# A mixture-of-experts trunk: expert outputs go to DRAM by slot and are fetched per token, in place of products with the slot matrix

## The chip, the cores and the metric

The kernel runs on one core of one Trainium2 chip. The metric is the device time of one execution, in microseconds (us). The kernel before took 1487.02 us, the median of 3 runs (1486.68 to 1487.57).

## The reference, cut to what matters

A two-layer trunk: 256 tokens of width 1024, attention and a dense SwiGLU in layer 0, attention and a mixture of 8 experts in layer 1. The change is in the mixture alone:

```python
logits = (t @ w_router).astype(jnp.float32)
top_val, top_idx = lax.top_k(logits, TOP_K)              # TOP_K = 2
gates = jax.nn.softmax(top_val, axis=-1)
combine = jnp.sum(jax.nn.one_hot(top_idx, N_EXPERTS, dtype=jnp.float32) * gates[..., None], axis=1)
y = jnp.zeros_like(t)
for e in range(N_EXPERTS):                                # N_EXPERTS = 8, EXPERT_FF = 3584
    y = y + combine[:, e:e + 1].astype(t.dtype) * swiglu(t, w_gate_up[e], w_down[e])
```

A token needs only its two experts. Everything is float32 in and out.

## The kernel before, in words

**Precision.** Every float32 product on TensorE (PE) is done as three products of rounded parts: high by high, high by low, low by high (`product`, L1665 to L1667). So each weight unit of 1 MB (128 partitions by 2048 values) is read from DRAM by SyncE's queue (SP) into one of six buffers `raw`. ScalarE (ACT) rounds it into `whi` (`split_hi`, L612), VectorE (DVE) subtracts to get `wlo` (`split_lo`, L975). `whi` and `wlo` have three places each: ACT may write unit c only when PE has finished unit c-3, and a load waits until DVE has finished the unit six before it.

**An expert** has 42 units in 7 steps of 512 columns. In step j PE does two G units (gate), two U units (up), and the two D units (down) of step j-1. One unit is 12 matmuls of 128x512. Between G's first and second unit PE transposes the previous step's activations (L2206); they pass through banks 6 and 7, which ACT and DVE read out. Banks 0 and 1 collect the down products of an expert over all 7 steps, banks 2 to 5 hold gate and up sums. Expert 0 and expert 7 are written out, experts 1 to 6 are one loop on every engine. Four units of expert 7 are loaded early into spare tiles (`attn`, `tok`).

**Tokens by slot.** Each expert has 128 slots. DVE builds the slot matrix `slot_oh` (token by slot, one_hot, L1531). For experts 1 to 7 PE gets the slots' token numbers from it, GpSimd's queue (POOL) fetches these rows from a copy `hn_rows` in DRAM with an indirect DMA (L586) during the previous expert, and PE transposes them (L2143).

**The way back.** In step 1 of each expert PE transposes the slot matrix (L2237) and ACT copies it to `slot_ohT` (L931). When the expert is done, that is in step 0 of the next one, ACT copies banks 0 and 1 to `ye_hi` (`output_hi`, L892), DVE makes `ye_lo` (`output_lo`, L1541), PE multiplies by `slot_ohT` (`back`, L2119 and L2120: 8 matmuls of 128x512, four after the first U unit, four after the second), and DVE adds the four results to the residual `X`, scaled by each token's gate (`add_back`, L1555). After expert 7 the same is done once more, in the open.

There is a second pass (`ps` = 1) for the case that more than 128 tokens choose one expert. It is skipped by a branch when, as here, it isn't needed.

The order is written out by hand for each engine. A wait that isn't met holds all later work of that engine.

Of the kernel before, what the change touches and what calls it, by code (L numbers as in the profile page):

```python
# [19 lines left out]
P = 128  # L20
# [47 lines left out]
TB = len(TB_USES)  # L68

# [108 lines left out]
def tb_count(use):  # L178

    return TB_USES.index(use) + 1  # L180


def tb_bank(use):
    return 6 + tb_count(use) % 2
# [6 lines left out]
def build(nc, x, mem, positions, mix_norm_g, ffn_norm_g, mem_norm_g, w_mem_kv, w_out, w_in_a, b_forget, w_q_b,  # L191
          lambda_q1, lambda_k1, lambda_q2, lambda_k2, subln_g, kv_norm_g, w_kv_shared, w_gate_up_dense,
          w_down_dense, w_router, w_gate_up_moe, w_down_moe, final_norm_g, out):
    with ExitStack() as ctx:
# [99 lines left out]
        xg_rows = hn[:, 0, :]  # L294
# [66 lines left out]
        hn_saved = sem("hn_saved")  # L361
        rows_ready, rows_out, rows_in = sem("rows_ready"), sem("rows_out"), sem("rows_in")
# [142 lines left out]
        def _(pool):  # L505
# [78 lines left out]
            for e in range(1, N_EXP):  # L584
                pool.wait_ge(rows_out, e)
                pool.indirect_dma_start(xg_rows, None, hn_rows,  # L586
                                        bass.IndirectOffsetOnAxis(ap=row_of[:, 0:1], axis=0)).then_inc(rows_in, 16)


        @block.scalar  # L590
        def _(act):
# [284 lines left out]
            def experts_act(ps):  # L876
                ub = U_MOE + ps * N_EXP * MOE_UNITS
                tb = 2 + TB * N_EXP * ps
                hb = FFN_STEPS + MOE_STEPS * N_EXP * ps

                def halves(use, base, dst, done):

                    for i in range(2):
                        act.wait_ge(tb_ready, base + tb_count(f"{use}{i}"))
                        a.copy(dst[:, 4 * i:4 * i + 4, :],
                               bank[tb_bank(f"{use}{i}")][:].rearrange("p (c n) -> p c n", c=4)).then_inc(done, 1)

                def output_hi(e):

                    act.wait_ge(unit_used, ub + MOE_UNITS * e)  # L890
                    for i in range(2):
                        a.copy(ye_hi[:, 4 * i:4 * i + 4, :],  # L892
                               bank[i][:].rearrange("p (c n) -> p c n", c=4)).then_inc(ye_hi_ready, 1)

                def expert(e, turns, first=False, final=False):
# [6 lines left out]
                    def evac_T(j):  # L902
                        act.wait_ge(tb_ready, tb + TB * e + tb_count(f"T{j}") - (2 if final and j == MOE_STEPS - 1 else 0))
                        a.copy(h2T_hi[j % 2][:], bank[tb_bank(f"T{j}")][:]).then_inc(h2_hi, 1)  # L904
# [8 lines left out]
                    if not first:  # L913
                        output_hi(e)
# [4 lines left out]
                    for j in range(1, MOE_STEPS):  # L919
# [9 lines left out]
                        if j == 1:  # L929
                            act.wait_ge(tb_ready, tb + TB * e + tb_count("oneT"))  # L930
                            a.copy(slot_ohT[:], bank[tb_bank("oneT")][:, 0:SEQ]).then_inc(ohT_out, 1)  # L931
                    if not final:
                        halves("gather", tb + TB * e, xg_hi, xg_hi_ready)
# [5 lines left out]
                halves("gather", tb - tb_count("gather1"), xg_hi, xg_hi_ready)  # L939
# [21 lines left out]
        def _(dve):  # L961
# [542 lines left out]
            def combine_weights():  # L1504
# [11 lines left out]
                step(ins)  # L1516
                step(d.tensor_reduce(over[:, 0:1], bank[4][:, 64:64 + N_EXP], AX.X, ALU.max))
# [3 lines left out]
            def experts_dve(ps):  # L1521
                ub = U_MOE + ps * N_EXP * MOE_UNITS
                tb = 2 + TB * N_EXP * ps
                hb = FFN_STEPS + MOE_STEPS * N_EXP * ps
                xb = 2 * N_EXP * ps
                ab = 4 + 4 * N_EXP * ps
# [9 lines left out]
                def halves(use, count, hi, lo, ready, done):  # L1536

                    for i in range(2):
                        dve.wait_ge(ready, count + i + 1)
                        b = bank[tb_bank(f"gather{i}")] if use == "gather" else bank[i]  # L1540
# [3 lines left out]
                def output_lo(e):  # L1544

                    halves("output", 2 * (N_EXP * ps + e) - 2, ye_hi, ye_lo, ye_hi_ready, ye_lo_ready)

                def add_back(e, i):
# [3 lines left out]
                    dve.wait_ge(tb_ready, tb + TB * e - TB + tb_count(f"back{i}")  # L1552
                                - (2 if isinstance(e, int) and e == N_EXP else 0))
                    dve.wait_ge(x_added, ab + 4 * e - 4)
                    d.scalar_tensor_tensor(out=X[:, t, cols], in0=bank[tb_bank(f"back{i}")][:],  # L1555
                                           scalar=comb[:, t, bass.ds(e - 1, 1)], in1=X[:, t, cols],
                                           op0=ALU.mult, op1=ALU.add).then_inc(x_added, 1)

                def expert(e, turns, first=False, final=False):
# [6 lines left out]
                    def evac_T(j):  # L1566
                        dve.wait_ge(h2_hi, hb + MOE_STEPS * e + j + 1)
                        d.tensor_tensor(h2T_lo[j % 2][:], bank[tb_bank(f"T{j}")][:], h2T_hi[j % 2][:].bitcast(F32),
                                        ALU.subtract).then_inc(h2_lo, 1)

                    def mul(j):
# [3 lines left out]
                        if j >= 2:  # L1575
                            dve.wait_ge(tb_ready, tb + TB * e + tb_count(f"T{j - 2}"))
                        elif not first:
                            dve.wait_ge(tb_ready, tb + TB * e - TB + tb_count("T6"))
# [5 lines left out]
                    if not first:  # L1584
# [3 lines left out]
                    if not first:  # L1588
# [3 lines left out]
                    if not first:  # L1592
# [14 lines left out]

# [681 lines left out]
```

## Time and profile before

| | |
|---|---|
| runs | 1486.68, 1487.02, 1487.57 us |
| the profiled execution, own time | 1487.61 us |
| its span, first to last instruction | 1485.7 us |
| PE busy | 1440.2 us (97%) |
| DVE busy | 1177.9 us (79%) |
| ACT busy | 952.1 us (64%) |
| mean granted TensorE clock | 0.989 of 2.4 GHz |
| moved by DMA | 432.61 MB, 291 GB/s over the span |
| chain that ended last | PE 91%, DVE 5%, issue 1%, ACT 1% |

The experts take the part from about 485 us to 1472 us. A busy time of PE is the union of its matmuls, and a matmul's own duration overlaps that of the next one, since they are pipelined. What one matmul costs in a row of them is the distance between two starts. "Idle before" is the time in which the engine had nothing running before the group, with what ended it.

### The profile page before, as it was taken

Reading aid. Unit: us, or ns where it says so; the run is one execution under the profiler, and the core shown is the slowest. Engines: PE = TensorE matmul, PEld = TensorE weight load, DVE = VectorE, ACT = ScalarE, POOL = GpSimd, SP = SyncE. Lnnn points to the kernel's source line nnn. Section 1 sums busy time; section 2 is a strip of 40 time slices with the busy share of each in tenths; the row PEclk is TensorE's granted clock in tenths of the full one; section 3 lists DMA queues with packets and bytes.
Section 4 is the critical chain, followed back from the end, with each engine's and each line's share of the span. In section 5 each row is a group of like instructions: output and inputs, shape, how many; then the busy total and the mean of one; then the engine's idle time right before and its main releaser. Section 6 shows DMA issues by size and latency. Waiting matters only on the chain.

```text
span 1485.7 us, 20701 instructions
## 1 busy us (share of the span) xinstructions
PE 1440.2 (97%) x7727; PEld 1222.5 (82%) x7727; DVE 1177.9 (79%) x1053; ACT 952.1 (64%) x876; POOL 27.6 (2%) x59
## 2 busy tenths in 40 slices
PE   8999999999998999999999999999999999999995
PEld 6987999998887788788888878878888887887884
DVE  6675444547787798988988898898889888889885
ACT  5545343335466577777767767777777777777774
POOL 2000000000000000000000000000000000000000
PEclk9999999999999899999999999999999999999998
DMA  9644355564534799999999999999999999998891
GB/s 303 200 129 156 129 170 179 191 202 150 171 114 174 284 379 381 338 361 380 376 338 387 374 334 378 383 335 369 391 365 342 375 376 340 371 390 294 312 375 51
DMA packets 205195, 432.61 MB, mean 291 GB/s; under 512 B 7008, under 2 KB 54112, under 8 KB 205136
## 3 DMA queue, kind: packets, MB, share of 16 engines
q1 hardware_dynamic: 202592, 423.65, 79.7%
q0 software_dynamic: 2544, 8.16, 1.7%
q8 instruction: 38, 0.62, 0.2%
q14 instruction: 21, 0.17, 0.0%
HBM read 429.69 MB, written 2.10 MB: 291 GB/s over the span
## 4 chain that ended last, share of the span: by engine, by line
PE 91%; DVE 5%; issue 1%; ACT 1%; DMA 0%; DVEq 0%; ACTq 0%; POOLq 0%
PE bank L1665 28%; PE bank L1667 28%; PE bank L1666 28%; DVE wlo L975 3%; PE bank L2206 1%; DVE X L1555 1%; PE bank L1680 1%; PE bank L1948 1%; PE bank L2119 0%; PE bank L1784 0%; PE bank L2120 0%; PE bank L2143 0%; PE bank L1822 0%; PE bank L1803 0%; PE bank L1848 0%
## 5 line engine op out<-in xcount | busy, mean ns | idle before, releaser
L975 DVE TENSOR_TENSOR wlo<-raw,whi 128x2048 fp32r<-128x2048 f32 x397 | 907.8, 2290 | 176.7 <-ACT whi L612 175.2
L612 ACT CAST whi<-raw 128x2048 fp32r<-128x2048 f32 x397 | 758.2, 1915 | 210.3 <-PE bank L1667 210.3
L1665 PE MATMUL bank<-whi,op_hi 128*128 128x512 f32 (+1 forms) x1176 | 444.0, 378 | 7.8 <-DVE wlo L975 4.6
L1667 PE MATMUL bank<-whi,op_lo 128*128 128x512 f32 (+1 forms) x1176 | 435.4, 370 | 0.0
L1666 PE MATMUL bank<-wlo,op_hi 128*128 128x512 f32 (+1 forms) x1176 | 435.1, 370 | 0.0
L1665 PEld LDWEIGHTS bank<-whi,op_hi 128*128 128x128 f32 x1176 | 222.1, 189 | 51.3 <-DVE wlo L975 9.9
L1667 PEld LDWEIGHTS bank<-whi,op_lo 128*128 128x128 f32 x1176 | 221.9, 189 | 38.6
L1666 PEld LDWEIGHTS bank<-wlo,op_hi 128*128 128x128 f32 x1176 | 222.3, 189 | 35.4
L1665 PE MATMUL bank<-whi,h2T_hi 128*128 128x512 f32 x544 | 214.3, 394 | 1.0 <-DVE h2T_lo L1371 1.0
L1667 PE MATMUL bank<-whi,h2T_lo 128*128 128x512 f32 x544 | 212.1, 390 | 0.0
L1666 PE MATMUL bank<-wlo,h2T_hi 128*128 128x512 f32 x544 | 211.9, 389 | 0.0
L1665 PE MATMUL bank<-op_hi,whi 128*128 128x256 f32 x512 | 148.0, 289 | 3.0 <-DVE wlo L975 3.0
L1666 PE MATMUL bank<-op_lo,whi 128*128 128x256 f32 x512 | 146.9, 287 | 0.0
L1667 PE MATMUL bank<-op_hi,wlo 128*128 128x256 f32 x512 | 146.8, 287 | 0.0
L1667 PEld LDWEIGHTS bank<-whi,h2T_lo 128*128 128x128 f32 x544 | 102.1, 188 | 21.7
L1665 PEld LDWEIGHTS bank<-whi,h2T_hi 128*128 128x128 f32 x544 | 102.2, 188 | 21.5 <-DVE h2T_lo L1371 1.4
L1666 PEld LDWEIGHTS bank<-wlo,h2T_hi 128*128 128x128 f32 x544 | 102.2, 188 | 20.2
L1665 PEld LDWEIGHTS bank<-op_hi,whi 128*128 128x128 f32 x512 | 100.5, 196 | 5.1 <-DVE wlo L975 3.2
L1666 PEld LDWEIGHTS bank<-op_lo,whi 128*128 128x128 f32 x512 | 100.5, 196 | 0.4
L1667 PEld LDWEIGHTS bank<-op_hi,wlo 128*128 128x128 f32 x512 | 100.3, 196 | 0.0
L904 ACT CAST h2T_hi<-bank 128x512 fp32r<-128x512 f32 x56 | 32.9, 587 | 72.8 <-PE bank L2206 72.8
L804 ACT ACTIVATE prob<-bank 128x512 f32<-128x512 f32 x11 | 6.6, 597 | 87.3 <-PE bank L1667 87.3
(297 smaller groups left out, 854.2 us busy)
## 6 DMA issues: line engine op xcount, KB each, us to landing
raw<-in_w_gate_up_moe_dram SPq DMA_DIRECT2D x223, 1024.0 KB, 6.8
raw<-in_w_down_moe_dram SPq DMA_DIRECT2D x109, 1024.0 KB, 7.0
raw<-in_w_gate_up_dense_dram SPq DMA_DIRECT2D x22, 1024.0 KB, 5.2
raw<-in_w_down_dense_dram SPq DMA_DIRECT2D x11, 1024.0 KB, 5.0
raw<-in_w_in_a_dram SPq DMA_DIRECT2D x10, 1024.0 KB, 13.1
raw<-in_w_out_dram SPq DMA_DIRECT2D x8, 1024.0 KB, 5.1
raw<-in_w_kv_shared_dram SPq DMA_DIRECT2D x6, 1024.0 KB, 5.2
raw<-in_w_mem_kv_dram SPq DMA_DIRECT2D x4, 1024.0 KB, 6.3
```

The lines of the kernel that those rows point to most:

```text
L612: a.copy(whi[:, c % SPLIT, :], src).then_inc(hi_ready, 1)
L804: a.activation(gate_act[j % 2][:], bank[4 + 2 * (j % 2)][:], ACT.Silu).then_inc(silu_done, 1)
L904: a.copy(h2T_hi[j % 2][:], bank[tb_bank(f"T{j}")][:]).then_inc(h2_hi, 1)
L975: d.tensor_tensor(wlo[:, c % SPLIT, :], src, whi[:, c % SPLIT, :].bitcast(F32), ALU.subtract).then_inc(lo_ready, 1)
L1555: d.scalar_tensor_tensor(out=X[:, t, cols], in0=bank[tb_bank(f"back{i}")][:], scalar=comb[:, t, bass.ds(e - 1, 1)], in1=X[:, t, cols], op0 ...
L1665: m.matmul(dst, sh, mh, start=start and i == 0, stop=False)
L1666: m.matmul(dst, sh, ml, start=False, stop=False)
L1667: last = m.matmul(dst, sl, mh, start=False, stop=stop and i == n - 1)
L1680: last = m.transpose(bank[g][:, P * c:P * (c + 1)], hn[:, t, P * k:P * (k + 1)], ident[:])
L1948: m.matmul(bank[4 + 2 * n + h][:], ones_row, gain_row[n][:, 512 * h:512 * (h + 1)], start=True, stop=True).then_inc(gain_out, 1)
L2206: last = m.transpose(bank[tb_bank(f"T{j}")][:, P * c:P * (c + 1)], h2[j % 2][:, P * c:P * (c + 1)], ident[:])
```

## The change

Experts 0 to 6 no longer go back through PE. ACT copies banks 0 and 1 as they are into a row tile `ye_rows` (the half `hn[:, 1, :]`), and POOL's queue writes it to DRAM at `y_rows`, 128 rows of 4 KB for each expert. The routing computes for each token and each of its two choices a row number, expert * 128 + slot, and a share, the gate. Where the choice is expert 7, or lies beyond slot 128, both are zero. During expert 7 two pairs of indirect DMAs fetch each token's first and then its second row into `hn`, and DVE adds them to `X` with the shares, in steps 2 and 4 (`add_stored`, two operations of 128x1024 each). Expert 7's own rows still go back by the products. The diff runs through POOL, ACT, the routing and the experts on DVE, and PE, in this order. The transposes of the slot matrix stay for expert 7 alone, now in its last step. The second pass keeps the old way.

```diff
             for e in range(1, N_EXP):
                 pool.wait_ge(rows_out, e)
                 pool.indirect_dma_start(xg_rows, None, hn_rows,
                                         bass.IndirectOffsetOnAxis(ap=row_of[:, 0:1], axis=0)).then_inc(rows_in, 16)
+                pool.wait_ge(y_out, 2 * e)
+                pool.dma_start(y_rows[P * (e - 1):P * e, :], ye_rows).then_inc(hn_saved, 16)
+            pool.wait_ge(hn_saved, 16 * (NT + N_EXP - 1))
+            pool.wait_ge(route_ready, 1)
+            pool.wait_ge(xg_lo_ready, 2 * N_EXP)
+            for i in range(2):
+                if i:
+                    pool.wait_ge(x_added, 4 + NT)
+                for t in range(NT):
+                    pool.indirect_dma_start(hn[:, t, :], None, y_rows,
+                                            bass.IndirectOffsetOnAxis(ap=back_of[:, i, t:t + 1],
+                                                                      axis=0)).then_inc(back_in, 16)
...
+                def output_rows(e):
+                    act.wait_ge(unit_used, ub + MOE_UNITS * e)
+                    act.wait_ge(hn_saved, 16 * e + 16 * (NT - 1))
+                    for i in range(2):
+                        a.copy(ye_rows[:, 512 * i:512 * (i + 1)], bank[i][:]).then_inc(y_out, 1)
...
                     if not first:
-                        output_hi(e)
+                        if ps:
+                            output_hi(e)
+                        else:
+                            output_rows(e)
...
+                for i in range(2):
+                    ins = d.tensor_tensor(place[:, i], oh[:, i], rank[:, :, 0:N_EXP], ALU.mult)
+                step(ins)
+                chosen = top_f[:, :, 0:2].rearrange("p t i -> p i t")
+                step(d.tensor_reduce(slot_of[:], place[:], AX.X, ALU.add))
+                step(d.tensor_scalar(known[:], slot_of[:], float(P), None, ALU.is_lt))
+                step(d.scalar_tensor_tensor(out=known[:], in0=chosen, scalar=float(N_EXP - 1), in1=known[:],
+                                            op0=ALU.is_lt, op1=ALU.mult))
+                step(d.scalar_tensor_tensor(out=slot_of[:], in0=chosen, scalar=float(P), in1=slot_of[:],
+                                            op0=ALU.mult, op1=ALU.add))
+                step(d.tensor_tensor(slot_of[:], slot_of[:], known[:], ALU.mult))
+                d.tensor_copy(back_of[:], slot_of[:])
+                d.tensor_tensor(share[:], gates[:, :, 2:4].rearrange("p t i -> p i t"), known[:], ALU.mult)
...
+                def add_stored(i):
+                    dve.wait_ge(back_in, 16 * NT * (i + 1))
+                    dve.wait_ge(x_added, 4 + NT * i)
+                    for t in range(NT):
+                        d.scalar_tensor_tensor(out=X[:, t, :], in0=hn[:, t, :], scalar=share[:, i, t:t + 1],
+                                               in1=X[:, t, :], op0=ALU.mult, op1=ALU.add).then_inc(x_added, 1)
...
-                    if not first:
+                    if ps and not first:
                         output_lo(e)
                     lo("U", 0, 0)
                     lo("U", 0, 1)
-                    if not first:
+                    if ps and not first:
                         add_back(e, 0)
                         add_back(e, 1)
...
+                        if j in (2, 4) and final and not ps:
+                            add_stored(j // 2 - 1)
                         lo("D", j - 1, 0)
...
                         up("U", j, 0)
-                        if j == 0 and not first:
+                        if j == 0 and ps and not first:
                             back(e, (0, 1))
                         up("U", j, 1)
-                        if j == 0 and not first:
+                        if j == 0 and ps and not first:
                             back(e, (2, 3))
-                        if j == 1:
-                            for t in range(NT):
-                                last = m.transpose(bank[tb_bank("oneT")][:, P * t:P * (t + 1)],
-                                                   slot_oh[:, t, :].bitcast(F32), ident[:])
-                            last.then_inc(tb_ready, 1)
+                        if j == 1 and ps or j == MOE_STEPS - 1 and final and not ps:
+                            one_hot_transposes()
...
+                        if j == 1 and not ps and not first:
+                            pe.wait_ge(y_out, 2 * e)
                         if j:
                             down(j - 1, 0)
```

**VectorE at the start of experts 1 to 6.** In the kernel before its queue holds this from `output_lo` on (`wlo<-raw,whi` is one weight unit's `split_lo`; register rows cost nothing to speak of):

```order
L1541 TENSOR_TENSOR op_lo<-bank,op_hi 128x4x128 [waits ye_hi_ready] x2
L973 REGISTER_ALU
L975 TENSOR_TENSOR wlo<-raw,whi 128x2048 [waits hi_ready]
L973 REGISTER_ALU
L975 TENSOR_TENSOR wlo<-raw,whi 128x2048 [waits hi_ready]
L1552 ISA
L1554 REGISTER_ALU [waits tb_ready]
L1555 ISA [waits x_added]
L1555 SCALAR_TENSOR_TENSOR X<-bank,comb,X 128x512
L1555 SCALAR_TENSOR_TENSOR X<-bank,comb,X 128x512 [waits x_added,tb_ready]
L973 REGISTER_ALU
L975 TENSOR_TENSOR wlo<-raw,whi 128x2048 [waits hi_ready]
```

In the changed kernel the same place, from the second weight unit of the expert on, reads (L1033 is `split_lo`, L1659 the product of gate and up):

```order
L1033 TENSOR_TENSOR wlo<-raw,whi 128x2048 [waits hi_ready]
L1031 REGISTER_ALU
L1033 TENSOR_TENSOR wlo<-raw,whi 128x2048 [waits hi_ready]
L1031 REGISTER_ALU
L1033 TENSOR_TENSOR wlo<-raw,whi 128x2048 [waits hi_ready]
L1031 REGISTER_ALU
L1033 TENSOR_TENSOR wlo<-raw,whi 128x2048 [waits hi_ready]
L1652 ISA
L1653 REGISTER_ALU [waits unit_used]
L1658 ISA [waits silu_done]
L1659 TENSOR_TENSOR probT<-prob,bank 128x512 [waits tb_ready]
```

Two subtractions and four additions into `X` have left this stretch, and with them the waits for PE's products (tb_ready) between two weight units.

**VectorE in step 2 of expert 7.** The changed kernel has two new rows between a U unit and the D units:

```order
L1033 TENSOR_TENSOR wlo<-raw,whi 128x2048 [waits hi_ready] x3
L1648 TENSOR_TENSOR h2T_lo<-bank,h2T_hi 128x512 [waits h2_hi]
L1033 TENSOR_TENSOR wlo<-raw,whi 128x2048 [waits hi_ready]
L1636 SCALAR_TENSOR_TENSOR X<-hn,share,X 128x1024 [waits x_added,back_in]
L1636 SCALAR_TENSOR_TENSOR X<-hn,share,X 128x1024
L1033 TENSOR_TENSOR wlo<-attn,whi 128x2048 [waits hi_ready]
L1033 TENSOR_TENSOR wlo<-raw,whi 128x2048 [waits hi_ready]
L1659 TENSOR_TENSOR probT<-prob,bank 128x512 [waits tb_ready,silu_done,unit_used]
```

Before, the D unit in `attn` follows the U unit at once. The same pair stands once more in step 4.

**TensorE in step 0 of experts 1 to 6.** Before, between the last matmul of one U unit and the first of the next:

```order
L1667 MATMUL bank<-whi,op_lo 128x512
L2119 MATMUL bank<-op_hi,slot_ohT 128x512 [waits xg_lo_ready,ohT_out,ye_lo_ready]
L2120 MATMUL bank<-op_lo,slot_ohT 128x512
L2119 MATMUL bank<-op_hi,slot_ohT 128x512 [waits h2_lo]
L2120 MATMUL bank<-op_lo,slot_ohT 128x512
L2169 REGISTER_ALU
L1665 MATMUL bank<-whi,op_hi 128x512 [waits lo_ready]
```

In the changed kernel the four L2119 and L2120 rows are gone here and after the second U unit.

## Rows read from the trace of the kernel before

**Rows 1.** Windows: length, PE, PEld, DVE, ACT, POOL busy, clock, DMA share, GB/s.

```profile
510.00:600.00 90.00, 90.00 (x410) 74.47 (x409) 80.26 (x47) 67.33 (x45) 2.97 (x1) 1.00 1.02 379
700.00:725.00 25.00, 25.00 (x118) 20.77 (x117) 21.90 (x12) 18.52 (x15) 0.97 (x1) 1.00 1.04 396
740.00:862.00 122.00, 121.33 (x553) 99.81 (x552) 109.30 (x68) 89.24 (x62) 0.94 (x1) 1.00 1.00 365
```

**Rows 2.** Groups by line, PE, 500 to 1480 us: busy, mean ns, idle before.

```profile
L2119 PE MATMUL bank<-op_hi,slot_ohT 128*128 128x512 f32 x32 | 12.8, 400 | 2.4 <-DVE op_lo L1541 2.0 <-DVE X L1555 0.4
L2120 PE MATMUL bank<-op_lo,slot_ohT 128*128 128x512 f32 x32 | 12.5, 390 | 0.0
```

**Rows 3.** Timeline of PE, step 0 of expert 3: start us, us, instruction.

```profile
863.04 0.50 PE L1665 MATMUL bank<-whi,op_hi 128*128 128x512 f32 x1
...
865.93 0.39 PE L2119 MATMUL bank<-op_hi,slot_ohT 128*128 128x512 f32 x1
...
866.84 0.39 PE L1665 MATMUL bank<-whi,op_hi 128*128 128x512 f32 x1
...
869.56 0.39 PE L2119 MATMUL bank<-op_hi,slot_ohT 128*128 128x512 f32 x1
...
870.47 0.50 PE L1665 MATMUL bank<-whi,op_hi 128*128 128x512 f32 x1
...
873.33 0.60 PE L2206 MATMUL bank<-ident,probT 128*128 128x128 f32 x4
874.60 0.50 PE L1665 MATMUL bank<-whi,op_hi 128*128 128x512 f32 x1 [0.67 <-DVE wlo L975]
874.94 0.40 PE L1666 MATMUL bank<-wlo,op_hi 128*128 128x512 f32 x1
```

**Rows 4.** Timeline of PE, the same place in expert 0.

```profile
507.80 0.60 PE L2206 MATMUL bank<-ident,probT 128*128 128x128 f32 x4
...
508.56 0.39 PE L1666 MATMUL bank<-wlo,op_hi 128*128 128x512 f32 x1
```

**Rows 5.** Timeline of PE, slot matrix transposes in expert 7.

```profile
1371.11 0.39 PE L1667 MATMUL bank<-whi,op_lo 128*128 128x512 f32 x1
...
1371.80 0.39 PE L1666 MATMUL bank<-wlo,h2T_hi 128*128 128x512 f32 x1
```

**Rows 6.** Timeline of DVE, step 0 of expert 3.

```profile
860.69 4.49 DVE L975 TENSOR_TENSOR wlo<-raw,whi 128x2048 fp32r<-128x2048 f32 x2 [0.20 <-ACT whi L612]
866.80 1.41 DVE L1555 SCALAR_TENSOR_TENSOR X<-bank,comb,X 128x512 f32<-128x512 f32 x2 [1.62 <-PE bank L2120]
...
870.34 1.41 DVE L1555 SCALAR_TENSOR_TENSOR X<-bank,comb,X 128x512 f32<-128x512 f32 x2
...
872.26 4.49 DVE L975 TENSOR_TENSOR wlo<-raw,whi 128x2048 fp32r<-128x2048 f32 x2
```

**Rows 7.** Timelines of DVE and PE, step 2 of expert 7.

```profile
1385.17 2.29 DVE L975 TENSOR_TENSOR wlo<-attn,whi 128x2048 fp32r<-128x2048 f32 x1
...
1388.41 0.39 PE L1665 MATMUL bank<-whi,h2T_hi 128*128 128x512 f32 x1
```

**Rows 8.** Groups by line, DVE: the nearest operations to the new ones.

```profile
L1499 DVE TENSOR_TENSOR op_lo<-hn,op_hi 128x1024 fp32r<-128x1024 f32 x1 | 1.2, 1219 | 0.0
...
L1653 DVE SCALAR_TENSOR_TENSOR hn<-X,stat,gain 128x512 f32<-128x512 f32 x2 | 1.4, 747 | 0.0
```

**Rows 9.** Timeline of DVE, expert 0's fourth unit, first after the routing.

```profile
499.11 2.29 DVE L975 TENSOR_TENSOR wlo<-raw,whi 128x2048 fp32r<-128x2048 f32 x1 [1.05 <-ACT whi L612]
```

**Rows 10.** DMA issues: KB each, median us to landing.

```profile
hn_rows<-hn POOLq DMA_DIRECT2D x2, 512.0 KB, 7.2
...
hn<-hn_rows,row_of POOLq DMA_INDIRECT x7, 7.1
```

**Rows 11.** Weight loads (L430), 620 to 1350 us.

```profile
DMA to landing us min/median/max: 5.0/7.0/9.4
```

**Rows 12.** Waits of ACT in expert 3: us in total, times, longest.

```profile
ACT whi L612 <- PE bank L1667: 20.4, 31, 1.7
```

More of the change, by code:

```diff
@@ L68 @@
 TB = len(TB_USES)
+TB_USES0 = [f"T{j}" for j in range(6)] + ["gather0", "gather1", "T6"]
+TB0 = len(TB_USES0)
+TB_PASS0 = 2 + TB0 * N_EXP - 2 + 5
 FILL = list(np.cumsum([4, 4, 8, 4, 4, 8, 5, 4]))
@@ L175, in moe_pos, with tb_start, tb_turn, tb_count @@
     return base + 2 * (kind == "U") + a
[L178 to L184, printed above, removed]
+def tb_start(ps):
+    return 2 + TB_PASS0 * ps
+def tb_turn(ps):
+    return TB if ps else TB0
+def tb_count(ps, use, final=False):
+    if ps:
+        return TB_USES.index(use) + 1 - 2 * (final and (use == "T6" or use[:4] == "back"))
+    if use[:4] == "back":
+        return TB0 + int(use[4])
+    if use == "oneT":
+        return TB_USES0.index("gather0") + 1
+    return TB_USES0.index(use) + 1 - (final and use == "T6")
+def tb_bank(ps, use):
+    if ps:
+        return 6 + tb_count(1, use) % 2
+    if use[:4] == "back":
+        return 7 - int(use[4]) % 2
+    return 6 if use == "oneT" else 6 + int(use[-1]) % 2
 S1, R1 = N0, N0
@@ L293, in build @@
         hn_rows = nc.dram_tensor("hn_rows", (SEQ, D), F32).ap()
-        xg_rows = hn[:, 0, :]
+        xg_rows, ye_rows = hn[:, 0, :], hn[:, 1, :]
+        y_rows = nc.dram_tensor("y_rows", ((N_EXP - 1) * P, D), F32).ap()
+        place = sb("place", [P, 2, NT, N_EXP])
+        slot_of = sb("slot_of", [P, 2, NT])
+        known = sb("known", [P, 2, NT])
+        share = sb("share", [P, 2, NT])
+        back_of = sb("back_of", [P, 2, NT], I32)
         over = sb("over", [P, 2])
@@ L902, in evac_T @@
                     def evac_T(j):
-                        act.wait_ge(tb_ready, tb + TB * e + tb_count(f"T{j}") - (2 if final and j == MOE_STEPS - 1 else 0))
-                        a.copy(h2T_hi[j % 2][:], bank[tb_bank(f"T{j}")][:]).then_inc(h2_hi, 1)
+                        act.wait_ge(tb_ready, tb + turn * e + tb_count(ps, f"T{j}", final))
+                        a.copy(h2T_hi[j % 2][:], bank[tb_bank(ps, f"T{j}")][:]).then_inc(h2_hi, 1)
                     def silu(j):
@@ L928, in expert @@
                         hi("D", j - 1, 1)
-                        if j == 1:
-                            act.wait_ge(tb_ready, tb + TB * e + tb_count("oneT"))
-                            a.copy(slot_ohT[:], bank[tb_bank("oneT")][:, 0:SEQ]).then_inc(ohT_out, 1)
+                        if j == 1 and ps:
+                            one_hot_T(e)
                     if not final:
-                        halves("gather", tb + TB * e, xg_hi, xg_hi_ready)
+                        halves("gather", tb + turn * e, xg_hi, xg_hi_ready)
+                    elif not ps:
+                        one_hot_T(e)
                     hi("D", MOE_STEPS - 1, 0)
@@ L1591, in expert @@
                     lo("G", 1, 0)
-                    if not first:
+                    if ps and not first:
                         add_back(e, 2)
@@ L2193, in h2_transposes @@
                         pe.wait_ge(mul_done, hb + MOE_STEPS * e + j + 1)
[L2195 removed]
+                        if j == MOE_STEPS - 1 and not ps:
+                            pe.wait_ge(*((ohT_out, 1) if final else (xg_lo_ready, xb + 2 * e + 3)))
+                        elif not ps:
+                            pe.wait_ge(h2_lo, hb + MOE_STEPS * e + max(j - 1, 0))
+                        elif j == 0:
                             pe.wait_ge(x_added, ab + 4 * e)
                         elif j == 2:
[L2198 removed]
+                            pe.wait_ge(ohT_out, yb + e + 1)
                         elif j == MOE_STEPS - 1 and final:
```

67 lines of the change are left out of this document (38 added, 29 removed).

## The prediction, written before the changed kernel ran

> **What bounds the kernel now.** I read the windows first. Inside the experts PE is busy for 121.3 of 122 us at full granted clock, while DVE has 109.3, ACT 89.2 [rows 1]. So PE's order sets the time there, and work taken off PE is worth its full price, as long as DVE, ACT and the loads keep ahead. Next I read the groups by line, to find what leaves PE: 32 L2119 and 32 L2120, with a mean of 400 and 390 ns [rows 2]. This mean must not be used as a price. The timeline shows that four such matmuls take from 865.93 to 866.84, 0.91 us, so one costs 0.2275 us; the rest of its 0.39 overlaps the next one [rows 3]. Last I read the timelines at the start of an expert, since the change works there. DVE has more to do in that place than anywhere else: two subtractions, and four additions to X that wait for PE's products, 1.62 us idle in one go [rows 6]. It falls behind, and PE pays: the unit after the transposes starts late with 0.67 us idle [rows 3].
>
> **What leaves PE.** (a) The products of `back` for experts 0 to 6: 7 experts x 8 matmuls x 0.2275 = 12.7 us. Those of expert 7 stay. They stand between full units with no gap before or behind [rows 3], so all of it is on the path. (b) The transposes of the slot matrix: eight pairs become one. From the last product before the pair to the second behind it are 0.69 us [rows 5], where three steps without a pair would have only two distances, 0.455; a pair costs 0.235 us, 7 of them 1.7 us.
>
> **What leaves DVE, and so PE's wait.** Step 0 loses two subtractions, four additions and the wait between them. In expert 3 DVE's two units from 860.69 are done at 865.18. The third begins only after the wait and two additions, at 868.2, and after two more additions and a product the fourth begins at 872.26 [rows 6]. PE needs the third at 870.47 and gets it just then: that unit takes 2.86 us up to 873.33, where the one between 866.84 and 869.56 takes 2.72, so 0.14 us are lost. It needs the fourth after the transposes. From their start to the second matmul behind them are 1.61 us [rows 3]. Expert 0 has the same step with no way back in it, and there the distance is 0.76 us [rows 4]. That is a direct look at the changed order: 0.85 us go. Together 0.99 us an expert, and 6.9 us for seven. What is late next in this place? The unit before the first products is 2.89 us long (865.93 less 863.04, from the same timeline's start of that unit), because ACT's two copies of banks 0 and 1 stand before its cast. These copies remain, with another target, so this 0.15 us stays. After it ACT, not DVE, is the later one, and PE has its unit in time.
>
> **What is added to DVE in expert 7.** Two pairs of additions of 128x1024. The trace has none of that shape. A multiply-add of 128x512 takes 0.747 us, a subtraction of 128x1024 1.22 us [rows 8]; two of 128x512 back to back take 1.41 [rows 6]. Going by width, the two bounds are 2 x 1.22 = 2.44 and 4 x 0.705 = 2.82 us for a pair; I take 2.5, nearest to the row of full width. They stand in front of the D unit in `attn`. Before, this one is done at 1385.17 + 2.29 = 1387.46, and PE begins on it at 1388.41 [rows 7]: a lead of 0.95 us. With 2.5 us in front it is 1.55 us late. The lead comes back by itself before the next unit, since DVE needs 2.3 us for one and PE 2.72. So each pair costs PE about 1.6 us, the two 3.2 us. Bounds: 2.44 - 0.95 = 1.5 and 2.82 - 0.95 + some 0.3 us of semaphore and start = 2.2 a pair; and nothing below, if the lead in steps 2 and 4 were larger, which the rows don't show. So 0 to 4.4, I take 3.2.
>
> **What is added and hidden.** (c) The routing gets nine small operations on DVE; at 0.2 us each for those with a step behind them, some 1.6 us. The next unit's subtraction waits 1.05 us for ACT there before [rows 9], and PE has three units to work on, the first ones at a lower clock. I count 0, at most 0.55. (d) ACT writes two copies to another place: 0; one copy of `slot_ohT` an expert goes. (e) POOL gets seven stores and four fetches. A store of 512 KB took 7.2 us to land, an indirect fetch of the same size 7.1 [rows 10]. Rows are ready some 1.3 us after expert 7 starts, so the store lands at +9 and the first two fetches at about +18. DVE asks for them at about +36 (step 2). The second pair is asked for 34 us after the first, and needs some 10. Both are covered by 18 us or more; if a cover were gone, each us late would be one us of PE, because the additions hold DVE's queue. POOL has nothing else queued behind them. (f) PE's new wait for `y_out` before the first D unit concerns copies that were done a step earlier: 0. ACT's wait for the previous store is met an expert earlier: 0.
>
> **The loads.** Each expert now also writes 0.52 MB. Per 122 us the core moves 122 x 365 = 44.5 MB; it would be 45.05 MB in about 119 us, 379 GB/s. Is that to be had? Over 90 us of expert 0 and 1 it moved 379, over 25 us 396 [rows 1]. A load lands 5.0 to 9.4 us after its issue [rows 11], and ACT's cast never waits for one: its 20.4 us of waiting in an expert are for PE [rows 12]. Six buffers at 2.72 us, less the 1.5 units that ACT is ahead of DVE, leave some 12 us from issue to use, 3 more than the worst landing. A store adds 0.52 / 0.39 = 1.3 us to the landing of the units beside it. So I count 0, but this is the thinnest cover in the sum.
>
> On this the Trainium skill speaks against the change. "DMA: Bandwidth & Descriptors", section "Where 436 GB/s comes from", puts the HBM side at about 358 GB/s for one core and says that this side binds transfers between HBM and SBUF. By that rule the experts would be bound by memory already, and any added byte would be time. The trace doesn't agree: 365 GB/s over a whole expert and 396 over 25 us [rows 1].
>
> **The sum.** 12.7 + 1.7 + 6.9 - 3.2 = 18.1 us. The profiled execution's own time was 1487.61 us, of which the span is 1485.7; both fall by it, to 1469.5 and 1467.6. The median of the runs was 0.6 us lower than the profiled execution, so I predict 1469.0 us. The tail after expert 7 has the same work in the same order as before, and nothing is taken from it.
>
> **Rivals.**
> 1. *The loads become the bound.* The mechanism: DMA can't sustain more than the 365 GB/s that a whole expert shows. Then an expert takes 45.05 / 0.365 = 123.4 us in place of 122, in all of experts 0 to 6, 7 x 1.4 = 10 us slower: 1497 us. It decides from the point where the sustained rate is below 45.05 MB / 122 us = 369 GB/s. For it: DMA share is 1.00 or above in all three windows. Against it: 379 and 396 GB/s in two of them, with the same share, so the share doesn't tell that the engines are full [rows 1]; and no cast waits for a load. A rate between 369 and 379 would give back a part only, 1470 to 1487. 7 in 100 for both, 5 of these slower.
> 2. *Another engine is late in the same place.* The removal of `back` gives PE 1.8 us less to do while ACT still copies banks 0 and 1. If ACT's casts are then the last, the 0.99 us of waiting stays and the pair costs its upper bound: 12.7 + 1.7 - 4.4 = 10.0, 1477 us. For it: the 0.15 us that ACT already costs. Against it: expert 0's distance [rows 4], though there ACT has no copies to do. 14 in 100.
> 3. *The stored rows come too late.* If the fetch of 128 single rows takes several times the 7.1 us, or POOL's queue is held, DVE and PE stop in step 2. With 18 us of cover it would need a threefold time to cost anything, and 18 us more than the cover to cancel the gain: about 1480 if it is 11 us late. 3 in 100.
> 4. *The additions are hidden.* The lead of DVE recovers enough, or the pair is faster, and the 3.2 us aren't paid: 1466 us. 12 in 100.
>
> The forecast as it stands has 64 in 100, with its own range of 1467 to 1471.5. Within 0.2% (3 us, what a measurement of this kernel can tell from no change) of before lies only a thin part of rival 1. So faster 0.93, same 0.02, slower 0.05. The range from 1465.0 to 1476.0 leaves out rival 1, most of rival 3 and a part of rival 2.
>
> **What would show it.** Right: L2119-like products appear only 8 times after 500 us; the distance over the transposes in step 0 is 0.76 us in every expert; an expert's period is 119.1 us, 3 less; PE's waits for `wlo` at starts of experts are gone, and two new ones of about 1.6 us stand in expert 7 behind the pairs of 128x1024. Wrong: casts of ACT that wait for a DMA, a period above 121 us, or DVE waiting for a fetch in expert 7. If the period is right and only the end is off, the additions were mis-sized.

## The result, and the profile after

The changed kernel takes 1471.59 us, the median of 4 runs (1468.94 to 1471.91). The kernel before took 1487.04 us beside it (4 runs, 1486.68 to 1487.57). The ratio is 0.9888, with a 95% interval from 0.9876 to 0.9900: 15.4 us faster. The forecast was 1469.0 us, within 1465.0 to 1476.0. The profiled execution took 1471.91 us, where the sum gave 1469.5.

The page of the changed kernel, the span and the busy time of each engine:

```profile
span 1470.0 us, 20457 instructions
PE 1424.3 (97%) x7657; PEld 1210.9 (82%) x7657; DVE 1156.0 (79%) x1024; ACT 949.9 (65%) x869; POOL 40.0 (3%) x70
```

PE's busy time fell by 15.9 us (from 1440.2) and the span by 15.7. This looks as if only products had gone, and that would be a wrong reading: busy time hides PE's short waits. The transposes below count as 0.60 us busy whether the next unit starts 0.61 us after them, as here, or 0.35 us, as in d1 further down. So each part is read from distances.

PE at the start of expert 3, the place of [rows 3]. Units are counted as in the prediction, from the first U unit on. The rows are the first matmul of the second and of the third unit, the transposes, and the first two matmuls of the fourth unit.

```profile
861.21 0.39 PE L1747 MATMUL bank<-whi,op_hi 128*128 128x512 f32 x1
863.93 0.39 PE L1747 MATMUL bank<-whi,op_hi 128*128 128x512 f32 x1
866.65 0.60 PE L2299 MATMUL bank<-ident,probT 128*128 128x128 f32 x4
867.26 0.50 PE L1747 MATMUL bank<-whi,op_hi 128*128 128x512 f32 x1
867.60 0.40 PE L1748 MATMUL bank<-wlo,op_hi 128*128 128x512 f32 x1
```

Two units of 2.72 us with nothing between, then 0.61 us from the transposes to the next unit and 0.95 us to its second matmul. In [rows 3] the latter was 1.61 us, and in [rows 4], the model for the forecast, 0.76. DVE in the same place:

```profile
855.99 6.70 DVE L1033 TENSOR_TENSOR wlo<-raw,whi 128x2048 fp32r<-128x2048 f32 x3 [1.47 <-ACT whi L654]
864.32 0.69 DVE L1659 TENSOR_TENSOR probT<-prob,bank 128x512 f32<-128x512 f32 x1 [1.63 <-PE bank L1749]
864.92 2.28 DVE L1033 TENSOR_TENSOR wlo<-raw,whi 128x2048 fp32r<-128x2048 f32 x1
```

Three units stand in a row, ahead of PE. Then DVE waits 1.63 us for PE's last U product before it can multiply gate and up (L1659), and only behind that comes the subtraction of the fourth unit. It starts at 864.92, ends at 867.20, and PE's fourth unit starts at 867.26. So PE still waits here for DVE, if far less than in [rows 3]. The wait shows in the row of the weight load:

```profile
867.26 0.19 PEld L1747 LDWEIGHTS bank<-whi,op_hi 128*128 128x128 f32 x1 [0.25 <-DVE wlo L1033]
```

A period is read from the fetches of rows, one an expert. POOL's timeline before, and then after:

```profile
1188.71 0.95 POOL L586 DMA_INDIRECT hn<-hn_rows,row_of  x1 [121.18 <-DVE row_of L1604]
1310.82 0.94 POOL L586 DMA_INDIRECT hn<-hn_rows,row_of  x1 [121.16 <-DVE row_of L1604]
```

```profile
1175.39 0.99 POOL L616 DMA_INDIRECT hn<-hn_rows,row_of  x1 [81.80 <-DVE row_of L1684]
1294.69 0.99 POOL L616 DMA_INDIRECT hn<-hn_rows,row_of  x1 [81.80 <-DVE row_of L1684]
1331.58 0.55 POOL L619 DMA_DIRECT2D y_rows<-hn  x1 [35.89 <-ACT hn L942]
1338.16 2.65 POOL L627 DMA_INDIRECT hn<-y_rows,back_of  x1 [6.04 <-DMA y_rows<-hn]
1341.11 0.97 POOL L627 DMA_INDIRECT hn<-y_rows,back_of  x1 [0.30 <-issue]
1368.65 2.75 POOL L627 DMA_INDIRECT hn<-y_rows,back_of  x1 [26.57 <-DVE X L1636]
```

The period falls from 122.11 to 119.30 us. The last store is issued at 1331.58, the first two fetches at 1338.16 and 1341.11. Their median landing by the page's list of DMA issues, after the store and the fetch of an expert's tokens:

```profile
y_rows<-hn POOLq DMA_DIRECT2D x7, 512.0 KB, 6.3
hn<-hn_rows,row_of POOLq DMA_INDIRECT x7, 7.6
hn<-y_rows,back_of POOLq DMA_INDIRECT x4, 7.3
```

So the first rows are there by 1349. DVE adds them in step 2 of expert 7:

```profile
1363.70 2.30 DVE L1033 TENSOR_TENSOR wlo<-raw,whi 128x2048 fp32r<-128x2048 f32 x1 [0.69 <-ACT whi L654]
1365.91 2.48 DVE L1636 SCALAR_TENSOR_TENSOR X<-hn,share,X 128x1024 f32<-128x1024 f32 x2
1368.30 2.29 DVE L1033 TENSOR_TENSOR wlo<-attn,whi 128x2048 fp32r<-128x2048 f32 x1
```

There is no wait before the additions, and 17 us of cover (1349 to 1366). They delay the D unit in `attn`, and PE waits for it:

```profile
1370.73 0.47 PE L1747 MATMUL bank<-whi,h2T_hi 128*128 128x512 f32 x1 [1.29 <-DVE wlo L1033]
```

The unit before it began at 1366.56. It had 4.17 us instead of 2.72, so 1.45 are lost, and some 0.1 more in its first distance. The second pair costs the same. After 500 us PE's products with `slot_ohT` are these eight, of expert 7, where [rows 2] has 32 and 32 (by line, from 500 us on):

```profile
L2201 PE MATMUL bank<-op_hi,slot_ohT 128*128 128x512 f32 x4 | 1.9, 474 | 2.4 <-DVE op_lo L1613 2.0 <-DVE X L1627 0.4
L2202 PE MATMUL bank<-op_lo,slot_ohT 128*128 128x512 f32 x4 | 1.6, 393 | 0.0
```

The window of one expert, with the columns of [rows 1]:

```profile
740.00:860.00 120.00, 119.99 (x546) 98.90 (x546) 106.20 (x62) 89.77 (x61) 1.54 (x2) 1.00 1.02 379
```

The loads move 379 GB/s over 120 us, where [rows 1] had 365 over a whole expert. The Trainium skill, "DMA: Bandwidth & Descriptors", section "Where 436 GB/s comes from", gives about 358 GB/s per core and says that this side binds transfers between HBM and SBUF. This chip moved more for the length of an expert, with one core at work, and the measurement decides.

### The profile page after: what moved, and what is told of

The parts are those of the page before. It is cut to its first block, busy times and chain, and to the rows that moved or that the text cites. A ratio compares the mean times of both kernels' runs of the same rounds, so it can differ in the third digit from the quotient of the medians.

```text
span 1470.0 us, 20457 instructions
## 1 busy us (share of the span) xinstructions
PE 1424.3 (97%) x7657; PEld 1210.9 (82%) x7657; DVE 1156.0 (79%) x1024; ACT 949.9 (65%) x869; POOL 40.0 (3%) x70
## 4 chain that ended last, share of the span: by engine, by line
PE 93%; DVE 4%; ACT 2%; issue 1%; DMA 0%; DVEq 0%; ACTq 0%; POOLq 0%
PE bank L1747 29%; PE bank L1749 29%; PE bank L1748 28%; PE bank L2299 2%; DVE wlo L1033 1%; ACT whi L654 1%; PE bank L1866 0%; PE bank L2225 0%; PE bank L1904 0%; PE bank L1885 0%; PE bank L1930 0%; PE bank L1871 0%; PE bank L2201 0%; DVE X L1636 0%; DVE op_lo L1103 0%
## 5 line engine op out<-in xcount | busy, mean ns | idle before, releaser
L1033 DVE TENSOR_TENSOR wlo<-raw,whi 128x2048 fp32r<-128x2048 f32 x397 | 907.1, 2290 | 178.7 <-ACT whi L654 177.4
```

What stands on the lines that cost most here:

```text
L1033: d.tensor_tensor(wlo[:, c % SPLIT, :], src, whi[:, c % SPLIT, :].bitcast(F32), ALU.subtract).then_inc(lo_ready, 1)
```

## The experiments

Executions differ by up to 3 us before the experts, where the change does nothing (last section). So besides the median this section uses a stretch of the profiled execution, one for each kernel: from the cast of the routing (`top_f`) to the memset of `over`, DVE's first operation behind the expert sums. This is "the expert stage". Its parts are the time to the first fetch, six periods, and the end. Between the two executions of the changed kernel no part differs by more than 0.3 us; the end is less steady in others (m1 and c1 below).

| run | median us | ratio to before, 95% | expert stage | period | last fetch to end |
|---|---|---|---|---|---|
| before | 1487.04 | 1 | 995.67 | 122.15 | 165.90 |
| changed | 1471.59 | 0.9888 (0.9876 to 0.9900) | 979.16 | 119.30 | 166.34 |
| a1 changed again | 1471.90 | 0.9897 (0.9880 to 0.9913) | 979.16 | 119.28 | 166.60 |
| d1 DVE's part alone | 1481.57 | 0.9956 (0.9940 to 0.9973) | 988.67 | 121.01 | 165.69 |
| p1 PE's part alone | 1485.66 | 0.9983 (0.9973 to 0.9992) | 993.28 | 121.77 | 165.65 |
| m1 one wait moved | 1471.01 | 0.9885 (0.9868 to 0.9901) | 979.41 | 119.14 | 167.64 |
| c1 copies split | 1469.37 | 0.9871 (0.9855 to 0.9887) | 978.08 | 119.06 | 166.98 |
| n1 no additions | 1468.07 | 0.9872 (0.9856 to 0.9889) | 976.02 | 119.31 | 163.40 |
| s1 additions in halves | 1466.84 | 0.9864 (0.9848 to 0.9881) | 976.15 | 119.32 | 163.36 |
| r1 three stores | 1470.54 | 0.9879 (0.9862 to 0.9895) | 979.12 | 119.30 | 166.36 |
| b1 three edits | 1466.25 | 0.9850 (0.9837 to 0.9863) | 973.81 | 118.87 | 163.64 |

Medians are of 4 runs each, b1's of 5 and p1's of 10. The kernel before had 1487.61 beside a1, m1, s1 and n1, 1487.86 beside d1, p1, r1 and c1, and 1487.75 beside b1. The seven fetches bound six periods. The column is the mean of the last five; the first is some 0.6 us shorter in every kernel. d1, p1 and n1 leave out or shrink work, as said below, so their output isn't that of the reference.

### The changed kernel again

> The changed kernel once more, as it is, so that the next three have it beside them on the same chip. The profiled execution of it spans 1470.0 us; 2.4 us of the forecast gain are missing. Theory A says 1.3 to 1.5 us of them sit in the start of experts 1 to 6 (2.83 us gained in each, in place of 3.05) and 0.8 us came before the experts, where the change does nothing and executions differ. So here the periods of the experts stay at 119.3 us, while the time before the experts may be up to 1 us different, and the median lies between 1469 and 1472 us.

Its expert stage is the same as the changed kernel's to 0.01 us, while the profiled execution is 2.8 us shorter (1469.14 against 1471.91). The whole difference lies before the experts, and it is more than the 1 us that was expected. So 1 or 2 us between two medians say nothing here, and the stage does.

### One wait of DVE's product moved (m1)

```diff
     def mul(j):
-        dve.wait_ge(unit_used, ub + moe_pos("U", j, 1) + 1 + MOE_UNITS * e)
         dve.wait_ge(silu_done, hb + MOE_STEPS * e + j + 1)
         ...
+        dve.wait_ge(unit_used, ub + moe_pos("U", j, 1) + 1 + MOE_UNITS * e)
         d.tensor_tensor(h2[j % 2][:], gate_act[j % 2][:], bank[3 + 2 * (j % 2)][:],
```

> The order of the three waits ahead of VectorE's product of gate and up is turned, so that the wait for TensorE's last up unit comes last. Theory A: in the looped experts register instructions stand between this wait and the product, and delay it by 0.19 us against expert 0, which is written out (0.61 us from the last matmul's start to the product, against 0.42); the fourth weight unit and with it TensorE is late by that in step 0. So the distance from the transposes in step 0 to the next matmul falls from 0.61 to 0.42 us in experts 1 to 6, the period from 119.3 to 119.1 us, and the time by 6 x 0.19 = 1.1 us. Rival: the 0.19 us come from ScalarE's copies earlier in the step; then nothing changes.

PE in step 0 of expert 3:

```profile
866.51 0.60 PE L2299 MATMUL bank<-ident,probT 128*128 128x128 f32 x4
866.94 0.50 PE L1747 MATMUL bank<-whi,op_hi 128*128 128x512 f32 x1
```

0.43 us, where the changed kernel has 0.61 and expert 0 has 0.42. The six periods together fell by 1.05 us, 0.17 each. The transposes were not late: they follow the matmul before them by 0.23 us in both kernels. Late was the unit behind them, since its subtraction stands in DVE's queue behind the product of gate and up. From the start of PE's last U matmul to that product are 0.62 us in the changed kernel and 0.43 in m1. In experts 1 to 6, which are a loop, the order has two instructions between the wait for PE and the product, L1653 (which carries that wait) and L1658. The views leave such rows out, but the trace file has them. L1653 starts at 864.14 and L1658 at 864.22, the product at 864.32. In m1 the two corresponding rows are done 3.1 us ahead of the product, while DVE waits. In expert 7, which is written out and has no such instructions there, the same edit makes the distance longer, 0.52 in place of 0.42, and in expert 0 0.49.

The 1.05 us of the six periods don't show in the stage, since its end took 1.3 us longer. Of these, 0.9 lie between the last unit's last matmul and the end of the last addition, where the granted clock was lower (last section); 0.3 lie in the idle time between the last addition and the memset.

### The additions in halves (s1) and not at all (n1)

```diff
-    if j in (2, 4) and final and not ps:
-        add_stored(j // 2 - 1)
+    if j in (2, 3, 5, 6) and final and not ps:
+        add_half(2 * (2, 3, 5, 6).index(j))         # 128x512, ahead of a U unit
     lo("U", j, 1)
     ...
     lo("D", j - 1, 0)
+    if j in (2, 3, 5, 6) and final and not ps:
+        add_half(2 * (2, 3, 5, 6).index(j) + 1)     # 128x512, ahead of a D unit
```

This is s1, in short; n1 drops the fetches and `add_stored`, with the waits that counted them.

> The four additions of 128x1024 in expert 7 are cut into eight of 128x512, one ahead of the second up unit and one behind the first down unit in each of steps 2, 3, 5 and 6. Theory A: TensorE pays only for what goes beyond VectorE's lead of 0.95 us and its own pauses of 0.4 to 0.7 us; an addition of 0.7 us fits in. So both waits of 1.3 to 1.6 us of TensorE in expert 7 go, and the time falls by 3.1 us (1.5 at least). Rival: what expert 7 lost comes from the fetches (their traffic, or GpSimd's queue) and not from the additions; then it stays, or spreads over four steps.

> Leaves out the fetch of the stored rows and their additions to X, so that only expert 7's rows reach the output; the stores remain. Theory A: the same time as with the additions cut in halves, 3.1 us less than the changed kernel, since fetches that land in time cost nothing. Rival: the fetches cost something of their own (more than 0.5 us below the kernel with halves).

The stage falls by 3.0 us in s1 and by 3.1 in n1. So spread in eight halves the additions cost nothing that shows, and in pairs they cost all that leaving them out would bring. The fetches cost nothing of their own that shows (0.1 us between the two). A half of s1, in expert 7:

```profile
1360.01 0.74 DVE L1645 SCALAR_TENSOR_TENSOR X<-hn,share,X 128x512 f32<-128x512 f32 x1
```

0.74 us fit into the idle time that DVE has before nearly every unit (0.42 or 0.69 us for ACT's cast) plus its lead of 0.95; the view of waits has none of PE from 1330 to 1445 us.

### Each part alone (d1, p1)

d1 is the kernel before without `output_lo` and the additions in step 0; the eight products stay, and PE's waits for what is left out are turned into waits that are met:

```diff
     lo("G", 0, 1)
-    if not first:
-        output_lo(e)
     lo("U", 0, 0)
     lo("U", 0, 1)
-    if not first:
-        add_back(e, 0)
-        add_back(e, 1)
     lo("G", 1, 0)
-    if not first:
-        add_back(e, 2)
-        add_back(e, 3)
     mul(0)
```

p1 is the kernel before with the eight products cut to two columns; all of DVE's work stays:

```diff
-    one_pass(bank[tb_bank(f"back{i}")][:].rearrange("p (c n) -> p c n", c=4), oneT, oneT,
-             ye_hi[:, 4 * h:4 * h + 4, :], ye_lo[:, 4 * h:4 * h + 4, :], True, True)
+    b = bank[tb_bank(f"back{i}")]
+    one_pass(b[:, 0:2], oneT, oneT, ye_hi[:, 4 * h, 0:2], ye_lo[:, 4 * h, 0:2], True, True)
```

> The kernel before, with VectorE's part of the way back left out for experts 0 to 6 (the subtractions to ye_lo and the additions to X; their rows don't reach the output), while TensorE still does all its products. Theory A: this alone removes TensorE's wait for the fourth weight unit in step 0, 0.85 + 0.14 us an expert, less the 0.19 us of register instructions that stay in the loop: periods fall from 122.15 to about 121.3 us, the time by 6 us. Rival: TensorE would wait there anyway, for ScalarE's copies; then the gain is under 2 us.

> The kernel before, with TensorE's products of the way back shrunk from 512 columns to 2 for experts 0 to 6 (what is added to X is then not theirs), while VectorE does all its subtractions and additions. Theory A: a matmul of the way back is worth 0.2275 us only if VectorE can follow. VectorE's extra 4.1 us in step 0 remain, so TensorE reaches the fourth unit earlier and waits longer for it: the gain of 1.8 us an expert is mostly eaten, 0 to 0.6 us an expert and 0 to 4 us in all. Rival, the two gains simply add: 12 us less.

In d1 the wait after the transposes is gone (PE, first transpose and next unit):

```profile
870.75 0.60 PE L2198 MATMUL bank<-ident,probT 128*128 128x128 f32 x4
871.10 0.48 PE L1657 MATMUL bank<-whi,op_hi 128*128 128x512 f32 x1
```

In p1 it has grown (PE in the same place, with the wait in brackets):

```profile
872.24 0.60 PE L2210 MATMUL bank<-ident,probT 128*128 128x128 f32 x4
873.46 0.50 PE L1665 MATMUL bank<-whi,op_hi 128*128 128x512 f32 x1 [0.62 <-DVE wlo L975]
```

The distance is 1.22 us, and another 0.47 us wait for `wlo` stands at 869.34. The products of two columns aren't free. The first four:

```profile
865.15 0.17 PE L2119 MATMUL bank<-op_hi,slot_ohT 128*128 128x2 f32 x1
865.18 0.25 PE L2120 MATMUL bank<-op_lo,slot_ohT 128*128 128x2 f32 x1
865.29 0.25 PE L2119 MATMUL bank<-op_hi,slot_ohT 128*128 128x2 f32 x1
865.40 0.25 PE L2120 MATMUL bank<-op_lo,slot_ohT 128*128 128x2 f32 x1
865.51 0.49 PE L1665 MATMUL bank<-whi,op_hi 128*128 128x512 f32 x1
```

They take 0.36 us where those of 512 columns take 0.91. So p1 takes some 1.1 us an expert from PE and not 1.82, and of these only 0.38 came through, since DVE was now what ended the boundary.

d1 brings more than was expected: 1.13 us a period, to 121.01 and not 121.3, and 7.0 us in the stage. Its distance after the transposes is 0.35 us, less than the 0.61 of the changed kernel. PE still has four products between the second and the third unit, and these 0.91 us give DVE the time to be ready for the fourth.

DVE's part alone brings 1.13 us a period, p1's part of PE's work 0.38, the pair of transposes 0.24 (worked out from [rows 5], no run has it alone): 1.75 in all, where the change has 2.84. Had the 0.72 us that p1 left on PE come through in full, it would be 2.47. So the parts are worth at least 0.4 us an expert more together than singly, and at most 1.1.

### Three stores for one (r1)

```diff
-    pool.dma_start(y_rows[P * (e - 1):P * e, :], ye_rows).then_inc(hn_saved, 16)
+    for y in [y_rows] + y_spare:
+        pool.dma_start(y[P * (e - 1):P * e, :], ye_rows).then_inc(hn_saved, 16)
```

> The changed kernel, which writes each expert's rows three times, twice of them to DRAM that nobody reads (1.05 MB more an expert). Theory A: loads land some 3 us later beside the stores, and the cover is some 3 to 5 us, so the periods stay at 119.3 us, within 0.3. Rival 1 of the prediction, the loads are near their bound: 1.05 MB at 380 GB/s would make each period 2.8 us longer, 17 to 19 us in all, and casts would wait for DMA. In expert 7 the fetches start some 2 to 5 us later, which 20 us of cover hide.

The window of an expert, and the landing of the loads and of the two spare stores:

```profile
740.00:860.00 120.00, 119.99 (x547) 98.91 (x546) 106.24 (x62) 90.04 (x61) 2.60 (x4) 1.00 1.03 387
```

```profile
raw<-in_w_gate_up_moe_dram SPq DMA_DIRECT2D x223, 1024.0 KB, 7.6
y_spare<-hn POOLq DMA_DIRECT2D x14, 512.0 KB, 9.1
```

One more MB an expert raises the rate to 387 GB/s, and the period stays at 119.30 us. From 620 to 1320 us the loads land in 7.8 us at the median and 11.7 at the most, where the changed kernel has 7.1 and 9.8; the expected 3 us is more than the median moved. The fetches of expert 7 start 5.9 us later (1344.05 against 1338.16), somewhat more than expected, and DVE doesn't wait for them. Rival 1 is excluded up to this rate. How much more would fit was not tried.

### ACT's second copy on DVE (c1)

```diff
     # ScalarE
-    for i in range(2):
-        a.copy(ye_rows[:, 512 * i:512 * (i + 1)], bank[i][:]).then_inc(y_out, 1)
+    a.copy(ye_rows[:, 0:512], bank[0][:]).then_inc(y_out, 1)
     # VectorE, after lo("G", 0, 1)
+    elif not first:
+        dve.wait_ge(hn_saved, 16 * e + 16 * (NT - 1))
+        dve.wait_ge(unit_used, ub + MOE_UNITS * e)
+        d.tensor_copy(ye_rows[:, 512:D], bank[1][:]).then_inc(y_out, 1)
```

> The changed kernel with the second of the two copies of an expert's rows done by VectorE, which waits for ScalarE in that place anyhow. Theory A: the 0.10 and 0.15 us that the second and third weight unit of step 0 take too long come from ScalarE's two copies ahead of its casts; with one copy less there the third unit is in time, and the period falls by 0.2 us to 119.1, the time by 1.4 us. Rival: they come from something else at the start of an expert (the wait for the gathered rows), then nothing changes.

The period falls by 0.25 us, the stage by 1.1, since its end took 0.6 us longer. The first units of expert 3 start at 854.48, 857.20 and 859.92 (two times 2.72), where the changed kernel has 855.52, 858.34 and 861.21 (2.82 and 2.87): the 0.25 us that ACT's two copies cost. The distance after the transposes stays at 0.61 us, so this is another loss than the one of m1.

### The three edits together (b1)

m1, s1 and c1 in one kernel.

> The changed kernel with all three edits: additions in halves over four steps of expert 7, the second copy of the rows on VectorE, and the turned order of waits ahead of the product of gate and up. If the three gains add (3.0 us from the halves, 0.25 us an expert from the copy, 0.17 us an expert from the order), the period is 118.9 us and from the routing to the end of the sums there are 3.0 + 7 x 0.25 + 6 x 0.17 = 5.8 us less than the changed kernel's 979.2: 973.4. The median would be about 1465.5 us. Rival: copy and order remove the same lateness of VectorE, and only the larger counts; then the period is 119.05 and the stretch 974.4 us.

The period is 118.87, 0.43 below the changed kernel's, and 0.25 + 0.17 = 0.42 were measured singly. The stage is 5.35 us shorter. The median, 1466.25 us, is the lowest here, and the kernel is faster than the one before by 1.50% (interval 1.37 to 1.63). Against s1 the medians tell nothing apart, the stages do (2.3 us). The expected 973.4 us of the stage was missed by 0.4.

## Why the prediction was right, and where its sizes were off

The mechanism and the sign were as forecast. Against a sum of 18.1 us the expert stage gained 16.5 and the profiled execution 15.7. By the steps:

- **Six boundaries in the loop: 2.83 us each, not 3.05.** The sum took 1.82 for products, 0.235 for the pair and 0.99 for waits. Measured are the six periods, 732.19 us before and 715.23 after: 16.96 in place of 18.3. This is the term that was mis-sized, the wait taken as gone in full: "There the distance is 0.76 us. That is a direct look at the changed order: 0.85 us go" [rows 4]. It was 0.95, so 0.66 went. Expert 0 is written out and experts 1 to 6 are a loop, with register instructions between the wait and the product. The part on the order said that register rows cost nothing to speak of. Behind a wait that is met last they cost 0.17 to 0.19 us (m1). So the sentence "After it ACT, not DVE, is the later one" was wrong for the fourth unit, and two of the prediction's signs were not met in the loop: 0.95 us in place of 0.76, and a wait for `wlo` that stays. The remaining 0.03 lies within ACT's part, 2.82 and 2.87 after for 2.75 and 2.89 before.
- **The boundary to expert 7: 3.0 us.** From the last fetch to the transposes of step 1 are 68.94 us before and 65.95 after. This expert is written out, and there the model of expert 0 held (0.42 us after the transposes, as there).
- **The parts don't stand alone.** The forecast priced products and waits apart and added them. Their sum holds to 0.2 us an expert, but they can't be had singly at these prices: PE's part gives 0.38 us of the 1.1 that p1 takes away, while DVE's part alone gives 1.13 where the sum has 0.99. The sentence "work taken off PE is worth its full price, as long as DVE, ACT and the loads keep ahead" was right by its condition only; at the boundary it was not met before.
- **The additions in expert 7: 3.1 us, forecast 3.2** (n1, s1). The pair takes 2.48 us, the value taken was 2.5. The loss is 1.45 us in the one unit, some 1.55 with the first distance. The "0.3 us of semaphore and start" in the upper bound stands in no row; here PE starts 0.14 us after the subtraction's end (1370.59 to 1370.73).
- **Nine routing operations: 0, as forecast.** DVE's fourth unit of expert 0 starts 18.40 us after the routing's cast (500.27 less 481.87), before 18.06, and PE doesn't wait for it. From the cast to the first fetch are 97.60 us, before 97.58. The pair of transposes that went from expert 0 (0.25) was offset by the granted clock. It came back to full about a matmul later, and the transposes of the first step stand at +27.02 from the cast in place of +26.75. In the repeat they stand at +26.89.
- **The one pair that stays** has moved to the last step of expert 7 and costs 0.28 us there. The end after it is longer by 0.03.
- **Sum of the stage:** 17.0 + 3.0 - 3.1 - 0.3 - 0.1 = 16.5. The other 0.8 us between 16.5 and 15.7 lie ahead of the experts, where the two profiled executions reach the routing's cast at 481.05 and 481.87; the repeat of the same kernel reaches it at 479.06.
- **Loads, stores, fetches: all hidden, as forecast** (r1 for the loads, POOL's timeline for the rest). The casts don't wait for a DMA; the loads land in 4.9 to 9.8 us.
- **Rival 2** was partly true. ACT is late in that place, but by 0.25 us for two units and not by the whole 0.99 (c1). The forecast named it, as 0.15 us; the two rows give 0.17 (2.89 less 2.72), and the unit before it was late as well.
- **Slips in the text on record:** the window of 90 us lies in expert 0 alone, seven pairs at 0.235 us are 1.6 and not 1.7, and the period of 119.1 us missed by 0.2.

What stays open: the clock's share. No experiment made it rise or fall on purpose.

## What to carry to other kernels

At the place where two engines are late in turn, price the parts together: the work taken off the bound engine comes through only as far as the next engine's queue has become shorter there, and one part alone may bring a third of what it takes away (p1). Take a model for a looped stretch from a looped stretch: here the code that is written out lacked the register operations that stood between a wait and its instruction. Where such a wait is met last, put it last. Side work costs the bound engine nothing in pieces shorter than the lead of the engine that does it (0.74 us under 0.95, s1), and in one piece what goes beyond the lead (1.5 of 2.48 us).

## What the runs showed of the hardware

**Register operations behind a wait** cost 0.17 to 0.19 us where the wait is the last to be met. Moving the wait behind them gains 0.17 us a period, and costs 0.07 to 0.1 us where the code has no register operations (m1, experts 0 and 7).

**The granted clock before the experts** isn't the same in two executions of one kernel. The first 60 us of the span, before, after and in the repeat; the clock is the third column from the right:

```profile
0.00:60.00 60.00, 53.86 (x363) 46.45 (x364) 37.75 (x59) 34.47 (x54) 10.35 (x40) 1.00 0.90 276
```

```profile
0.00:60.00 60.00, 52.07 (x360) 46.06 (x360) 37.86 (x59) 34.15 (x53) 10.34 (x40) 0.94 0.89 276
```

```profile
0.00:60.00 60.00, 52.15 (x370) 46.15 (x371) 37.74 (x59) 34.49 (x54) 10.31 (x40) 0.97 0.91 277
```

The same work at 1.00, 0.94 and 0.97 of 2.4 GHz. The routing's cast comes at 481.05, 481.87 and 479.06, so this one window doesn't set the order alone. Over the eleven profiled executions the cast lies between 479.00 and 482.10 us. That is more than any one of the small edits brings.

**The clock after the last unit.** PE's last eight products come after short idle times. In b1, 10 us that hold the last three of them:

```profile
1450.00:1460.00 10.00, 1.16 (x3) 0.43 (x2) 3.36 (x8) 2.90 (x8) 0.00 (x0) 0.50 0.02 5
```

A granted clock of 0.50, 1.2 GHz. In m1 the distances between these products are 0.4 to 0.6 us, in the changed kernel 0.24 to 0.34. From the last unit's last matmul to the end of the last addition m1 takes 7.0 us, the changed kernel 6.1. Together with 0.3 us more of idle time before the memset this hides what the moved wait gained. Why the clock fell in some executions was not found.

**Memory** gave 387 GB/s over 120 us with one core at work, and the loads of 1 MB still landed in 7.6 us at the median (r1).
